# Second up step of the MLP as seven Strassen products instead of eight plain ones

## The reference

```python
xn = rms_norm(x, p['norm1_w'])
aq, ak, av, mq, mk, mv, mo, mi, mf = split_in(xn @ p['w_in'])
...   # differential attention heads, mLSTM heads
x = x + jnp.concatenate([att, ml], axis=-1) @ p['w_out']
hn = rms_norm(x, p['norm2_w'])
x = x + jnp.square(jax.nn.relu(hn @ p['w_up'])) @ p['w_down']
```

## Time and profile before

| | us |
|---|---|
| median of 3 runs | 2402.58 (2401.92 to 2403.91) |
| profiled execution | 2401.66, span 2400.1 |
| TensorE busy | 2389.1 |
| VectorE busy | 1748.3 |
| ScalarE busy | 1086.5 |
| GpSimd busy | 299.2 |

### The profile page before, as it was taken

The page is one execution under the profiler, slowest core; times in us unless marked ns, Lnnn a source line. Parts: engine busy times, 40 slices in busy tenths (PEclk is TensorE's granted clock), DMA queues, the critical chain, the costliest instruction groups (busy, mean ns, idle before and its releaser), DMA issues.

```text
span 2400.1 us, 48706 instructions
## 1 busy us (share of the span) xinstructions
PE 2389.1 (100%) x18938; PEld 2364.0 (98%) x18938; DVE 1748.3 (73%) x2566; ACT 1086.5 (45%) x1708; POOL 299.2 (12%) x392
## 2 busy tenths in 40 slices
PE   8999999999999999999999999999999999999999
PEld 8999999999999999999999999999999999999999
DVE  7466565666656674488887787888888888888887
ACT  5445353443535453364444444444544444444443
POOL 0000000000000100012122222212311110111110
DMA  5323323232332433424444443444856556665654
GB/s 184 118 87 113 99 88 105 92 104 80 114 102 85 142 112 109 158 90 146 148 142 145 154 153 140 143 147 142 294 172 173 166 165 171 181 181 173 172 165 123
DMA packets 116112, 334.75 MB, mean 139 GB/s; under 512 B 13048, under 2 KB 20856, under 8 KB 116000
## 3 DMA queue, kind: packets, MB, share of 16 engines
q1 hardware_dynamic: 88352, 222.14, 29.0%
q0 software_dynamic: 26208, 106.60, 15.2%
q10 hardware_dynamic: 1440, 4.47, 0.5%
HBM read 274.07 MB, written 59.09 MB: 139 GB/s over the span
## 4 chain that ended last, share of the span: by engine, by line
PE 98%; DVE 1%; issue 0%; ACT 0%; DMA 0%; DVEq 0%; ACTq 0%
PE psum L919 52%; PE psum L682 35%; PE psum L707 1%; PE psum L838 1%; PE psum L996 1%; PE psum L764 1%; PE psum L958 1%; PE psum L966 1%; PE psum L962 1%; PE psum L778 1%; PE psum L807 1%; PE psum L722 0%; PE psum L740 0%; PE psum L738 0%; DVE forms_lo L1903 0%; PE psum L756 0%
## 5 line engine op out<-in xcount | busy, mean ns | idle before, releaser
L682 PE MATMUL psum<-act_tiles,w_hi 128*128 128x272 f32 x4544 | 758.5, 289 | 0.0
L919 PE MATMUL psum<-forms_hi,wp_lo 128*128 128x272 f32 x3416 | 711.4, 288 | 0.0
L919 PE MATMUL psum<-forms_hi,wp_hi 128*128 128x272 f32 x3416 | 709.0, 287 | 1.5 <-DVE wp_lo L1889 1.5
L919 PE MATMUL psum<-forms_lo,wp_hi 128*128 128x272 f32 x3416 | 709.8, 287 | 0.0
L682 PEld LDWEIGHTS psum<-act_tiles,w_hi 128*128 128x128 f32 x4544 | 642.7, 188 | 7.0 <-issue 4.0
L919 PEld LDWEIGHTS psum<-forms_lo,wp_hi 128*128 128x128 f32 x3416 | 541.6, 189 | 0.0
L919 PEld LDWEIGHTS psum<-forms_hi,wp_hi 128*128 128x128 f32 x3416 | 537.5, 188 | 1.9 <-issue 1.1
L919 PEld LDWEIGHTS psum<-forms_hi,wp_lo 128*128 128x128 f32 x3416 | 535.3, 188 | 0.0
L682 PE MATMUL psum<-act_tiles,w_lo 128*128 128x272 f32 x2272 | 468.8, 288 | 0.0
L1295 ACT ACTIVATE wp_hi<-ws 128x1024 fp32r<-128x1024 f32 x244 | 259.3, 1063 | 438.9 <-PE psum L919 231.0
L1889 DVE TENSOR_TENSOR wp_lo<-ws,wp_hi 128x1024 fp32r<-128x1024 f32 x244 | 303.7, 1245 | 113.2 <-ACT wp_hi L1295 108.8
(11 more groups left out here) (333 smaller groups left out, 2201.8 us busy)
## 6 DMA issues: line engine op xcount, KB each, us to landing
wa<-in_wpairs SPq DMA_DIRECT2D x248, 512.0 KB, 3.7
w_raw<-in_wstream SPq DMA_DIRECT2D x291, 256.0 KB, 2.8
hidden_forms<-hid POOLq DMA_DIRECT2D x32, 952.0 KB, 4.0
hid<-hidden_forms POOLq DMA_DIRECT2D x31, 952.0 KB, 8.1
out_yT<-cbuf POOLq DMA_DIRECT2D x62, 272.0 KB, 6.6
form_raw<-hidden_forms SPq DMA_DIRECT2D x7, 1088.0 KB, 7.6
res<-in_xT POOLq DMA_DIRECT2D x16, 272.0 KB, 4.0
kc_sb<-in_kcT POOLq DMA_DIRECT2D x8, 512.0 KB, 4.1
```

The source lines that it names most:

```text
L682: last = nc.tensor.matmul(out[0:m, half, :], w[:, w_slot, col:col + m], x[:, half * HB:(half + 1) * HB], start=start and n_ == 0, stop=sto ...
L919: return nc.tensor.matmul(BANKS[i], weights[:, w, s], form[:, k, :], start=STARTS[i] and k == 0 and n_ == 0, stop=k == HALF - 1 and n_ == ...
```

## The change

Step 1 becomes a step of seven products. Its first three weight sums are made by VectorE in rounds 48, 50 and 52 of w_out (`SECOND_SUM`). The second plain step and its own orders (`second_up` on ScalarE and VectorE) are gone; the general `up` now begins at step 1, with the last pieces of the forms put into it where `first` is true. t2, form 5's raw sum and the low parts of forms 1 and 2 move up to stand beside step 0. The first and the last up step stay plain. The rest are counts: there is one more combined step, so `combined(p)` falls away and the offsets of the counters change.

```diff
+SECOND_SUM = {48: 0, 50: 1, 52: 2}
-FORM_AT = {0: 0, 1: 6, 2: 4, 3: 5, 4: 2, 5: 7, 6: 3}
+FORM_AT = {0: 0, 1: 4, 2: 5, 3: 6, 4: 2, 5: 7, 6: 3}
...
 # TensorE
                 for group_ in PLAIN_GROUPS:
-                    plain_products(0, group_)
+                    plain_products(group_)
...
-                for group_ in PLAIN_GROUPS:
-                    plain_products(1, group_)
-
+                for i in range(7):
+                    product(Step(1), i, 2 * FORM_AT[i])
...
 # SyncE
                 load_a21(Step(2))
+                load_a22(Step(2))
                 load_a11(Step(2))
                 load_a12(Step(2))
-                load_a22(Step(2))
...
 # ScalarE
                 x_form(6, b22)
-                plain_split(4)
-                plain_split(5)
-                act.wait_ge(x_term, 2)
+                wp_split(Step(1), 0)
+                act.wait_ge(x_term, 3)
+                act.wait_ge(product_done, 3)
+                x_form(1, t2_raw)
                 x_form(2, form_lo_raw(2))
                 x_form(3, form_lo_raw(3))
+                wp_split(Step(1), 1)
                 square(Step(0), cbuf[:, 0, 0, :], 0, c11_done, Step(1))
                 square(Step(0), cbuf[:, 1, 0, :], 4, c21_done, Step(1))
-                plain_split(6)
-                plain_split(7)
+                wp_split(Step(1), 5)
                 square(Step(0), cbuf[:, 0, 1, :], 7, c12_done, Step(1))
-                square(Step(0), cbuf[:, 1, 1, :], 6, c22_done, Step(1))
...
+                wp_split(Step(1), 2)
 
                 def up(p):
...
                     wp_split(p, 3)
                     copy_y(p)
                     wp_split(p, 4)
+                    if first:
+                        square(Step(0), cbuf[:, 1, 1, :], 6, c22_done, Step(1))
+                        act.wait_ge(form_lo_ready, 2 * FORM_AT[1] + 2)
+                        x_form(5, form_lo_raw(5))
                     wp_split(p, 6)
...
 # VectorE
                         plain_lo(FIRST_LO[r])
+                    if r in SECOND_SUM:
+                        (sum_1, sum_2, sum_3)[SECOND_SUM[r]](Step(1))
...
                 def up(p):
...
                     wp_lo_part(p, 3)
+                    if first:
+                        form_lo_part(3, FORM_AT[3])
                     from_u(p)
                     wp_lo_part(p, 4)
                     sum_4(p)
+                    if first:
+                        form_lo_part(5, FORM_AT[5])
                     if not end:
                         sum_1(p + 1)
```

More of the change, by code:

```diff
@@ L430, in load_a21 @@
                 def load_a21(p):
-                    if p.reg is None and p.first == 2:
-                        sp.wait_ge(wp_lo_ready, len(PLAIN_W) + 2)
-                    elif p.reg is None and p.first == PAIRS:
+                    if p.reg is None and p.first == PAIRS:
                         sp.wait_ge(wp_lo_ready, PLAIN_LO + 1)
@@ L439, in load_a22 @@
                 def load_a22(p):
-                    if p.reg is None and p.first == 2:
-                        sp.wait_ge(wp_lo_ready, len(PLAIN_W) + 4)
-                    elif p.reg is None and p.first == PAIRS:
+                    if p.reg is None and p.first == PAIRS:
                         sp.wait_ge(wp_lo_ready, PLAIN_LO + 3)
@@ L451, in load_a12 @@
                 def load_a12(p):
-                    if p.reg is None and p.first == 2:
-                        sp.wait_ge(wp_lo_ready, len(PLAIN_W) + 3)
-                    elif p.reg is None and p.first == PAIRS:
+                    if p.reg is None and p.first == PAIRS:
                         sp.wait_ge(wp_lo_ready, PLAIN_LO + 2)
@@ L1396, in copy_y @@
                     act.wait_ge(product_done, (p * 7 + 1).v)
+                    if not (p.reg is None and p.first == 1):
+                        act.wait_ge(u_done, (p + (-1)).v)
                     if p.reg is None and p.first == PAIRS:
@@ L1447, in up @@
                         wp_split(p + 1, 5)
[L1448 removed]
+                    square(p, cbuf[:, 1, 1, :], 6, relu_ready, p * 3 + (-2))
                     square(p, cbuf[:, 0, 0, :], 0, c11_done, p + 1)
@@ L1472, in last_up @@
                     wp_split(q, 2)
[L1473 to L1476 removed]
+                    square(p, cbuf[:, 0, 1, :], 7, v_done, p)
+                    square(p, cbuf[:, 1, 1, :], 6, relu_ready, Step(3 * LAST_UP - 2))
+                up_pairs(act, lambda p: last_up() if p.reg is None and p.first == LAST_UP else up(p))
                 def refill(t, part):
@@ L1894, in reused @@
                         dve.wait_ge(wp_lo_ready, PLAIN_LO - 1)
-                    elif not (p.reg is None and p.first == 2):
+                    elif not (p.reg is None and p.first == 1):
                         dve.wait_ge(wp_lo_ready, split_count(p + (-1), i).v)
@@ L1990, in _, with plain_c @@
                 dve.wait_ge(x_term, 2)
+                dve.wait_ge(x_acc, 2 * KT)
+                nc.vector.tensor_tensor(t2_raw[:], b22, form_lo_raw(2), ALU.add).then_inc(x_term, 1)
                 form_lo_part(6, 3, b22)
-                def plain_c(p, a, b, bank, count, done):
-                    dve.wait_ge(product_done, 7 * p + count)
+                dve.wait_ge(x_term, 3)
+                nc.vector.tensor_tensor(form_lo_raw(5), b21, t2_raw[:], ALU.subtract).then_inc(x_term, 1)
+                def plain_c(a, b, bank, count, done):
+                    dve.wait_ge(product_done, count)
@@ L2006, in _ @@
-                dve.wait_ge(x_term, 2)
-                dve.wait_ge(x_acc, 2 * KT)
-                nc.vector.tensor_tensor(t2_raw[:], b22, form_lo_raw(2), ALU.add).then_inc(x_term, 1)
-                dve.wait_ge(x_term, 3)
-                nc.vector.tensor_tensor(form_lo_raw(5), b21, t2_raw[:], ALU.subtract).then_inc(x_term, 1)
-                plain_lo(6)
-                plain_lo(7)
-                plain_c(0, 0, 1, bank_z, 6, c12_done)
-                plain_c(0, 1, 1, bank_4, 7, c22_done)
@@ L2067, in up @@
                 def up(p):
-                    end = p.reg is None and p.first == LAST_UP - 1
+                    first, end = p.reg is None and p.first == 1, p.reg is None and p.first == LAST_UP - 1
                     wp_lo_part(p, 3)
+                    if first:
+                        form_lo_part(3, FORM_AT[3])
                     from_u(p)
@@ L2140, in last_up @@
                     wp_lo_part(q, 2)
-                up_pairs(dve, lambda p: second_up() if p.reg is None and p.first == 1 else last_up() if p.reg is None and p.first == LAST_UP else up(p))
+                up_pairs(dve, lambda p: last_up() if p.reg is None and p.first == LAST_UP else up(p))
                 def refill(t, part):
```

114 lines of the change are left out of this document (39 added, 75 removed).

## The result

The changed kernel takes 2406.26 us (median of 22 runs, 2405.16 to 2407.58), the kernel before 2402.53 us in the same series (22 runs, 2401.81 to 2403.91): 3.7 us more, a ratio of 1.0016 with a 95% interval of 1.001 to 1.0021. The forecast was 2406.4 (range 2401.5 to 2408.7). The profiled execution took 2405.89 us, 4.2 more than that of before (2401.66).

The account below looks back on a forecast made before the run. The prediction took VectorE's queue to bound the changed stretch: waits of 6.9 us less 3.0 for 24 fewer matmuls gave +3.9, VectorE's total +3.6; the middle, +3.8 on 2402.58, gave 2406.4 us, range 2401.5 to 2408.7.

Parts of the forecast that it names:

- second sum: VectorE's total work from 1053.93 to the low part for product 2 of the third step: 44.1 us, giving +3.6 us.
- pitch: New products running one after the other into a single bank each: wider matmul spacing costs at most 0.13 us.
- collisions: GpSimd's additions on `hid` slowing VectorE instructions beside them: 2.3 us charged, 2.0 for the first string, 0.3 for the second.
- Rival A: VectorE's queue hides the added work and only the 24 fewer matmuls count: -3.0, 2399.6 us; chance 0.07.
- C: Each of six GpSimd additions blocks VectorE a full 0.77 us, 4.6 instead of 2.3: +6.1, 2408.7 us; chance 0.14.
- B: VectorE binds, but GpSimd's string costs nothing on the way to a product: +1.5, 2404.1 us; chance 0.15.
- GpSimd's string: GpSimd's four additions on `hid` after step 0's fourth square, about 1076: 2.0 us charged to VectorE.
- The waits one by one: TensorE waiting for late VectorE results from the first step's fourth group to the third step's product 2: 6.9 us.
- second string: GpSimd's next additions, about 1097, slowing VectorE beside them: 0.3 us charged.
- first sum: VectorE's queue laid out instruction by instruction: waits of 6.9 us less 3.0 saved by fewer matmuls, +3.9 us.

Follow-up runs that it names:

- light low parts: Changed kernel with low parts of weights of the second step and the third computed in 8 of 1024 columns only: 2400.7 us, ratio 0.9991.
- one sum twice: Changed kernel with the sum S1 of the third step made twice on VectorE, the second behind the first: 2407.35 us.
- evacuations first: Changed kernel with the evacuations of banks y and x moved ahead of form 1's low part in VectorE's list: 2406.36 us, ratio 1.0014.
- form 5 later: On top of fourth sum early: form 5's difference later, A21 of the third step loaded before A12, step 0's squares behind S1's high part: 2403.4 us.
- both runs without the string: Changed kernel with GpSimd's first four additions held until the third step's first product ends, or cut to 8 of 272 columns: 2404.42 and 2404.4 us.
- string at product 16: Changed kernel with GpSimd's additions of step 0 held until the third step's second product is done: 2405.84 us, ratio 1.0013.
- fourth sum early: Changed kernel with S4 also summed during w_out, GpSimd's first additions held to the third step's first product, A21 loaded last, VectorE reordered: 2404.11 us.

## Why the prediction was right, point by point

**The cause was right.** VectorE's total sets the time. It was 43.31 us busy of 44.00, the waits fell where its queue is late, none came in w_out, and none after 1098 in the up loop. The forecast's second sum can be laid beside the trace: its 41 instructions are all there (3, 10, 15 and 13 of the four kinds), and they run from 1054.11 to 1097.88, 43.8 us where 44.1 were forecast. That sum gave +3.6; waits and pitch together, less 3.0, are 3.3 in the profiles. The collisions took 0.35 us less than charged, and ScalarE 0.40 where 0.5 were. Making its work lighter (light low parts) or heavier (one sum twice) and reordering it (evacuations first, form 5 later) moved the time as that theory says. Rival A (the queue hides it, 2399.6) is out, and so is C (0.77 us an addition): the rows have at most 0.58. B, in which GpSimd's string costs nothing, is out as well: both runs without the string gained 1.9 us. B's time, 2404.1, is near what the kernel takes when that cost is taken away (2404.4).

**The waits one by one**, forecast against measured: fourth group of the first step 0.3 and 0.23; product 0 1.4 and 1.38; product 1 0.9 and 0.84; product 2 0.1 and 0.09; product 3 0.5 and none; product 4 0.5 and 0.10; product 5 none and 0.56; product 6 1.1 and 1.23; in the third step product 0 0.1 and 0.06, product 1 1.6 and 1.67, product 2 0.4 and none. In all 6.9 and 6.16.

**What was off.** Three small things. Of the collisions only 0.58 us fell on form 3's halves and 0.57 on form 5's, where the forecast had none on form 5's; so the 0.5 us at products 3 and 4 came at product 5 instead. As product 6 stands behind all of them, that changed the places and not the total. And the second string (1097.38) came after the last bound instruction had started (1096.66), so 0.3 us of collisions and the 0.4 at product 2 did not come. The collisions were 1.95 us where 2.3 were charged. And the single-bank pitch, put at 0.13 us at most, measured some 0.2 (light low parts). The second step of before begins at 1066.0, behind the pair that follows the one at 1065.51, and takes 24.0 us to 1090.0, not 24.1 from 1065.8; the 0.125 us a matmul are right.

**What the forecast left out, and what stays open.** By the waits alone the time should have risen by 3.2 us; it rose by 3.7, and in the profiles by 4.05 from the end of w_out to the last matmul. In the profile 0.75 us of that stands at the turn from the up to the down steps, where TensorE of before waited 0.73 and 1.08 us. In the changed kernel there are three waits, 0.28 at 1738.96 and 1.08 and 1.10 at these rows of TensorE's timeline:

```profile
1749.21 0.39 PE L909 MATMUL psum<-forms_hi,wp_hi 128*128 128x272 f32 x1 [0.92 <-DVE wp_lo L1864]
...
1751.91 0.51 PE L909 MATMUL psum<-forms_hi,wp_hi 128*128 128x272 f32 x2 [0.93 <-DVE wp_lo L1864]
```

Ahead of them ScalarE waited for a load of forms, and VectorE 0.85 us for ScalarE; in before neither waited there:

```profile
1732.80 2.12 ACT L1366 ACTIVATE forms_hi<-form_raw 128x1088 fp32r<-128x1088 f32 x2 [0.80 <-DMA form_raw<-hidden_forms]
```

Such a wait of ScalarE stands there in five of the nine profiled kernels of seven products (0.65 to 1.94 us) and in none of the three of eight. The waits at the turn, with the slower starts behind them, are 2.5 to 3.2 us in those five and 2.0 to 2.1 in the other four, 2.0 to 2.4 in the kernels of eight products. They don't follow the waits of the second step: with the string at product 16 they are 2.0, with the fourth sum early 3.0. Whether the change makes that load late more often, one profile each can't show.

So the forecast of +3.8 met +3.7 with 0.7 us too much for the waits in its first sum, and some 0.5 us that no term stood for: 0.2 of pitch and the rest, as far as the profiles show it, at the turn. The mechanism was right; that it came this close was in part luck, two errors of opposite sign.

**The clock** stayed at 1.00, as forecast; the longest pause was 1.57 us.

## What to carry to other kernels

When an engine is 98% busy over a stretch, don't ask only which instruction is late: add up what stands in its queue up to the last instruction that someone waits for, and compare with the time that the other engine needs. The single waits moved when the order changed; their sum stayed at 6.16 us as long as nothing left the queue (evacuations first). Fewer matmuls on an engine that is fed by another were worth nothing here until the feeding got shorter: 24 matmuls (3.0 us) were paid with 4.5 us more of VectorE's busy time (43.31 against 38.84 in the same 44 us) in a stretch with some 0.7 us to spare. An engine beside the path (GpSimd) cost the bound engine 1.9 us here by the moment at which it starts, and one semaphore value gave it back, since at the new moment the bound engine idled.

## What the runs showed of the hardware

After a pause of 2.12 us (evacuations first) the granted clock fell to 0.50, the 1.2 GHz level, some 0.4 us after TensorE had resumed; 15 matmuls then started 0.226 us apart instead of 0.125, and by 1076.2 the clock was back at 1.00. The 1.5 us so lost stand against waits that shrank: at products 5 and 6 they are 0.41 us together, in the changed kernel 1.63, and the sum is 6.16 us in both. So most of it took the place of waiting for VectorE. That it cost nothing is not shown: in 9 of the 11 runs of that kernel the mean clock of the run was 0.999, and the two at 1.000 were 2405.43 and 2405.7 us, two of the three shortest. With the sum made twice, whose pause is 2.42 us, the clock stayed at 1.00 in the profiled execution and was 0.999 in 3 of 11 runs, and these took 2408.06, 2409.21 and 2409.4 us, where the others had 2406.8 to 2408.3. In the changed kernel, whose longest pause is 1.57 us, the table shows 1.00. The longer pause saw the clock fall in fewer runs than the shorter, so the length of the pause alone does not decide it here.

In the collisions GpSimd lost more than VectorE: its addition took 1.5 to 1.8 us instead of 0.77, a VectorE instruction 1.80 instead of 1.22. The Trainium skill (SBUF — State Buffer, section Who interferes with whom) has the later of the two blocked fully for the other's length. The rows show less for VectorE, 0.58 us beside additions of 0.77. That need not speak against it: under the string VectorE's sum and the next operation start 1.73 us apart (1080.71 to 1082.44), GpSimd's additions 1.77 to 1.84, which is what one of each would take in turn if an addition kept VectorE out for some 0.6 us of its 0.77. That is an estimate from these rows; no run here tells the two apart.
